# Opening a two-block transformer by quarters: an earlier x, columns from PSUM, a moved filler, three weight units rounded ahead

## The reference

```python
cond = jax.nn.silu(c)
mod = (cond @ ada_w[l] + ada_b[l])[:, None, :]
sh1, sc1, g1, sh2, sc2, g2 = jnp.split(mod, 6, axis=-1)
h = rmsnorm(x, norm1_g[l]) * (1 + sc1) + sh1
proj = h @ w_in + b_in
```

## Time and profile before

| | |
|---|---|
| median of 3 runs | 1454.11 us |
| lowest and highest | 1453.11 and 1454.91 us |
| the profiled execution's own time | 1455.57 us |
| its span in the profile | 1453.8 us |
| TensorE busy | 1424.6 us (98%) |
| GpSimd busy | 1209.7 us (83%) |
| ScalarE busy | 758.7 us (52%) |
| VectorE busy | 718.3 us (49%) |
| moved by transfers | 313.35 MB, mean 216 GB/s |

### The profile page before, as it was taken

The page is one execution under the profiler, slowest core; times in us unless marked ns, Lnnn a source line. Parts: engine busy times, 40 slices in busy tenths (PEclk is TensorE's granted clock), DMA queues, the critical chain, the costliest instruction groups (busy, mean ns, idle before and its releaser), DMA issues.

```text
span 1453.8 us, 21473 instructions
## 1 busy us (share of the span) xinstructions
PE 1424.6 (98%) x7560; PEld 1193.2 (82%) x7560; DVE 718.3 (49%) x1555; ACT 758.7 (52%) x1279; POOL 1209.7 (83%) x984
## 2 busy tenths in 40 slices
PE   6999999999999999999999999999999999999997
PEld 4798777799988987778888888878888888788886
DVE  6863654766643754754566303454650044655202
ACT  4435775644444335765654445574654345655442
POOL 3799989898878987559898997967999977789995
PEclk9999999999999999999999999999999999999999
DMA  9994546678875986337675565644555656345561
GB/s 364 401 352 160 198 166 228 237 296 317 311 256 164 401 310 222 109 101 232 215 247 205 188 203 162 200 143 137 195 190 194 222 164 188 131 164 199 193 200 56
DMA packets 147651, 313.35 MB, mean 216 GB/s; under 512 B 11076, under 2 KB 31960, under 8 KB 147544
## 3 DMA queue, kind: packets, MB, share of 16 engines
q1 hardware_dynamic: 145504, 310.55, 62.2%
q10 hardware_dynamic: 2040, 1.42, 0.3%
HBM read 310.87 MB, written 1.06 MB: 215 GB/s over the span
## 4 chain that ended last, share of the span: by engine, by line
PE 86%; POOL 4%; DVE 4%; DMA 2%; ACT 2%; issue 1%; SPq 0%; POOLq 0%; DVEq 0%; ACTq 0%
PE bank L810 54%; PE bank L855 12%; PE bank L856 8%; POOL lo_units L747 4%; PE bank L853 3%; DMA raw_units<-in_w_ffn_out 1%; PE bank L1018 1%; ACT hi_units L1359 1%; PE bank L1002 1%; DMA raw_units<-in_w_ffn_tiles 1%; PE bank L988 1%; PE bank L891 1%; PE bank L1105 1%; PE bank L1034 1%; PE bank L1070 1%
## 5 line engine op out<-in xcount | busy, mean ns | idle before, releaser
L747 POOL TENSOR_TENSOR lo_units<-raw_units,hi_units 128x512 fp32r<-128x512 f32 (+3 forms) x928 | 1150.5, 1275 | 223.3 <-ACT hi_units L1359 222.1
L1359 ACT ACTIVATE hi_units<-raw_units 128x1024 fp32r<-128x1024 f32 (+1 forms) x470 | 482.8, 1030 | 404.7 <-PE bank L810 235.6
L810 PE MATMUL bank<-hi_units,turned 128*128 128x512 f32 (+3 forms) x1600 | 442.2, 391 | 5.9 <-DVE turned L1888 4.3
L810 PEld LDWEIGHTS bank<-hi_units,turned 128*128 128x128 f32 x1600 | 291.7, 189 | 57.7 <-DVE turned L1888 6.3
L856 PE MATMUL bank<-turned,lo_units 128*128 128x256 f32 x1024 | 288.1, 281 | 0.0
L810 PE MATMUL bank<-hi_units,turned_wide 128*128 128x512 f32 x992 | 274.6, 391 | 0.0
L855 PE MATMUL bank<-turned,hi_units 128*128 128x512 f32 x736 | 260.1, 398 | 0.0
L810 PE MATMUL bank<-lo_units,turned 128*128 128x512 f32 (+3 forms) x800 | 253.1, 383 | 0.8 <-POOL lo_units L747 0.5
L810 PEld LDWEIGHTS bank<-hi_units,turned_wide 128*128 128x128 f32 x992 | 185.3, 188 | 38.5 <-issue 0.5
L856 PEld LDWEIGHTS bank<-turned,lo_units 128*128 128x128 f32 x1024 | 194.2, 190 | 0.2
L810 PEld LDWEIGHTS bank<-lo_units,turned 128*128 128x128 f32 x800 | 150.0, 188 | 30.9 <-POOL lo_units L747 3.6
(11 more groups left out here) (256 smaller groups left out, 1288.1 us busy)
## 6 DMA issues: line engine op xcount, KB each, us to landing
ada_units<-in_ada_w SPq DMA_DIRECT2D x72, 512.0 KB, 7.2
raw_units<-in_w_ffn_tiles SPq DMA_DIRECT2D x72, 512.0 KB, 4.7
raw_units<-in_mlp_w_out SPq DMA_DIRECT2D x64, 512.0 KB, 3.2
raw_units<-in_mlp_w_tiles SPq DMA_DIRECT2D x56, 512.0 KB, 3.2
raw_units<-in_w_in SPq DMA_DIRECT2D x56, 458.0 KB, 9.9
raw_units<-in_w_in SPq DMA_DIRECT2D x48, 512.0 KB, 6.8
raw_units<-in_w_ffn_out SPq DMA_DIRECT2D x44, 512.0 KB, 3.8
raw_units<-in_moba_w_qkv SPq DMA_DIRECT2D x24, 512.0 KB, 3.7
```

Source lines behind the costliest of these rows:

```text
L747: pool.tensor_tensor(LO[:, s, b, 0:w], RAW[:, u["slot"], b, 0:w], HI_[:, s, b, 0:w].bitcast(F32), ALU.subtract).then_inc(lo_ready.sem, lo_ ...
L810: ins = pe.matmul(BANK[2 * c["pair"] + t][:, 0:w], (A[a] if A is BT else A[:, a])[:, part, t * P:(t + 1) * P], W[:, s, b, 0:w], start=(i = ...
L1359: act.activation(HI_[:, s, 0:n, 0:w], RAW[:, u["slot"], 0:n, 0:w], ACT.Copy)\
```

## The change

1. SP sends the two halves of x ahead of the unit (0, 0, 2) and not (0, 0, 3).
2. The columns are worked out as sums * gain + bias with one operand in PSUM each time. The gain is 1 for the shift; for the scale it is g, and the bias is (b + 1) * g, which one new operation, `first_constants`, makes from the tables behind the reciprocal on VectorE. The host's table has the gains spread out: 32 numbers to a partition where it was 24.
3. The filler between the turns and the first column sums goes behind them.
4. Behind the loop over the quarters, and ahead of the sine, ScalarE rounds units 8, 9 and 10 (`prep(11)`).

```diff
--- before.py
+++ after.py
@@ -470,8 +470,7 @@
     ZA, ZU, ZL, LF, F8 = (small(NT * HC) for _ in range(5))
     MX, NM, RS, RR = (small(48) for _ in range(4))
     STAT = small(24)
-    FIRST_BIAS, FIRST_GAIN = NM[:, 0:2 * KT], NM[:, 2 * KT:3 * KT]
-    BIASED, GAINED = RS[:, 0:2 * KT], MX[:, 0:KT]
+    FIRST_BIAS, FIRST_GAIN, FIRST_SCALED = NM[:, 0:2 * KT], NM[:, 2 * KT:4 * KT], RS[:, 0:2 * KT]
     MV, RSTD, NMR = small(4), small(2), small(2)
 
     BANK = [ctx.enter_context(nc.psum_tensor(f"bank{i}", [P, CW], F32)) for i in range(8)]
@@ -662,7 +661,7 @@
                     sp.wait_ge(unit_used.sem, unit_used.at(last_unit["branch", l, 1, "B"]))
                 if (l, c, i) == (0, 4, 0):
                     sp.dma_start(CON[:, n_early:n_const], dram["constants"][:, n_early:n_const]).then_inc(late_const_in, 16)
-                if (l, c, i) == (0, 0, 3):
+                if (l, c, i) == (0, 0, 2):
                     for t in range(NT):
                         sp.dma_start(X[:, t, :], dram["x"][0, t * P:(t + 1) * P, :]).then_inc(x_in[t], 16)
                 if (l, c) in FIRST_BANK:
@@ -1218,9 +1217,8 @@
                 ready = lambda g: (act_side, ("unit rows", g // 2))
                 turn(tag, O, range(4), 0, ready)
                 turn(tag, O, range(4), 1, ready)
-                keep_running(1, BANK[3])
                 column_sums(0)
-                keep_running(1, BANK[3])
+                keep_running(2, BANK[3])
                 for q in range(N_FIRST):
                     pe.wait_ge(turned_lo.sem, turned_lo.at((tag, q)))
                     unit(c0, q, HT)
@@ -1382,7 +1380,8 @@
             bank = BANK[(TQ, TP)[q % 2]]
             for k in (0, 1):
                 part = bank[:, k * S:(k + 1) * S]
-                ins = act.activation(part, part, ACT.Identity, scale=GAINED[:, 2 * q + k:2 * q + k + 1], bias=BIASED[:, 4 * q + 2 + k:4 * q + 3 + k])
+                ins = act.activation(part, part, ACT.Identity, scale=FIRST_SCALED[:, 4 * q + k:4 * q + k + 1],
+                                     bias=FIRST_SCALED[:, 4 * q + 2 + k:4 * q + 3 + k])
             ins.then_inc(act_side.sem, act_side.mark(("whole", q)))
             act.wait_ge(act_side.sem, act_side.at(("whole", q)))
             act.activation(HT[:, 2 * q:2 * q + 2, 0, :], bank[:, :].rearrange("p (k s) -> p k s", k=2), ACT.Copy)\
@@ -1652,7 +1651,7 @@
         act.dma_start(CON[:, 0:n_early], dram["constants"][:, 0:n_early]).then_inc(const_in, 16)
         act.wait_ge(c_in, 16)
         act.activation(CT, COND, ACT.Tanh, scale=0.5).then_inc(act_side.sem, act_side.mark("cond"))
-        act.dma_start(NM[:, 0:3 * KT], dram["first_columns"]).then_inc(first_in, 16)
+        act.dma_start(NM[:, 0:4 * KT], dram["first_columns"]).then_inc(first_in, 16)
         act.dma_start(RB[:, :], dram["rel_bias"].rearrange("l h r -> (l h) r")).then_inc(rel_in, 16)
         act.dma_start(POS[:, :], dram["positions"].rearrange("b (t p) -> (b p) t", p=P),
                       allow_slow_non_contiguous=True).then_inc(pos_in, 16)
@@ -1674,6 +1673,7 @@
                     if q == 0:
                         unit_rows(1)
                     prep(2 * q + 2)
+                prep(2 * N_FIRST + 3)
                 for what, dst in (("sin", SIN), ("cos", COS)):
                     act.wait_ge(rows.sem, rows.at(what))
                     act.activation(dst, dst, ACT.Sin).then_inc(act_side.sem, act_side.mark(what))
@@ -1931,12 +1931,17 @@
 
         def first_columns(q):
 
-            dve.wait_ge(first_in, 16)
             dve.wait_ge(product.sem, product.at(("columns", q)))
             cols = slice(4 * q, 4 * q + 4)
-            link(v.tensor_tensor(BIASED[:, cols], BANK[SB_[1]][:, cols], FIRST_BIAS[:, cols], ALU.add))
-            say(v.scalar_tensor_tensor(GAINED[:, 2 * q:2 * q + 2], BIASED[:, 4 * q:4 * q + 2], 1.0, FIRST_GAIN[:, 2 * q:2 * q + 2], ALU.add, ALU.mult),
-                ("columns", q))
+            sums = BANK[SB_[1]][:, cols]
+            link(v.tensor_tensor(sums, sums, FIRST_GAIN[:, cols], ALU.mult))
+            say(v.tensor_tensor(FIRST_SCALED[:, cols], sums, FIRST_BIAS[:, cols], ALU.add), ("columns", q))
+
+        def first_constants():
+
+            dve.wait_ge(first_in, 16)
+            scales = lambda a: a.rearrange("p (q four) -> p q four", q=N_FIRST)[:, :, 0:2]
+            link(v.scalar_tensor_tensor(scales(FIRST_BIAS), scales(FIRST_BIAS), 1.0, scales(FIRST_GAIN), ALU.add, ALU.mult))
 
         def across_norm(take, norm, next_tag):
 
@@ -2087,6 +2092,7 @@
             first_sum(0, kt)
         dve.wait_ge(act_side.sem, act_side.at(("root", ("n1", 0))))
         say(v.reciprocal(RR[:, 0:NT], RSTD), "inverse root")
+        first_constants()
         for kt in range(6, KT):
             first_sum(0, kt)
         for l in range(DEPTH):
@@ -2591,7 +2597,9 @@
     half = CW // 2
     cols = [np.concatenate([np.arange(D + q * half, D + (q + 1) * half), np.arange(q * half, (q + 1) * half)]) for q in range(N_FIRST)]
     first = np.stack([w[:, c].reshape(P, KT, CW) for c in cols])
-    columns = np.concatenate([b[c].reshape(4, P) for c in cols] + [g.reshape(KT, P)]).T
+    ones = np.ones((2, P), g.dtype)
+    gains = [np.concatenate([g.reshape(N_FIRST, 2, P)[q], ones]) for q in range(N_FIRST)]
+    columns = np.concatenate([b[c].reshape(4, P) for c in cols] + gains).T
     return {"in_ada_first": np.ascontiguousarray(first), "in_first_columns": np.ascontiguousarray(columns)}
 
 
```

## The result

The changed kernel takes a median of **1458.74 us** over 8 runs (1457.41 to 1459.40), the kernel before 1453.94 over 8 (1453.11 to 1454.91). The ratio is 1.0032, with an interval of 1.0021 to 1.0043: slower by 4.8 us, where 4.8 had been predicted. The profiled execution took 1458.59 us, its span 1456.8.

The account below looks back on a forecast made before the run. TensorE was taken to bound the kernel, with 86% of the chain of waits. The terms -1.45 + 5.4 - 0.55 + 1.4 gave +4.8 us on a median of 1454.11: 1458.9 us predicted, range 1453.0 to 1461.0 (the case's own 1456.5 to 1461.0).

Parts of the forecast that it names:

- x and the first constants: Opening: x one transfer sooner gains 0 (at worst 0.3 us lost); the added operation behind the reciprocal costs 0.
- The cover: Before the seventh sum: its 0.40 us wait for a transfer was to hide the added operation's 0.18 us.
- The opening: Filler moved and columns reworked: first columns 1.30 us sooner, 0.15 in the next quarter, -1.45 us; worse bound -0.9.
- the step: Filler and columns: ScalarE starts the first columns at 17.4 instead of 18.70, after unit 0's rounding.
- Six more operations held: VectorE before the first projection's drain: GpSimd's eight subtractions hold six more small operations, +5.4 us (3.6 to 6.3).
- The two short delays: Around unit 8: 0.30 us from drain end to its start and about 0.25 us for its low part go, -0.55 us.
- The half clock at unit 8: TensorE idles 6.3 us before unit 8, then runs at half clock: +1.4 us, between 0 and twice that.
- a shift at 55 us reaches the end unchanged: From 55 us on: TensorE passes on what the opening gains or loses, carried to the end unchanged.
- VectorE is held: Against the rival at L2064 to L2081 that VectorE is not held up further: 1452.1 or 1451.2 us, chance 0.13.
- GpSimd does not pause: Against the rival that GpSimd pauses as unit 9 or 10 is rounded later: +1.3 us, 1455.4, chance 0.09.
- VectorE does get its turn: Against the rival that VectorE waits at L2056 until 53.4: +1.5 us on top, 1460.4, chance 0.04.

Follow-up runs that it names:

- e4: The changed kernel without units 8 to 10 rounded ahead and with x back at its old place; 1452.24 us, 0.9983 of the kernel before.
- e1: The changed kernel with units 8 to 10 rounded after the sines again, so the opening alone; 1452.74 us, 0.9988 of the kernel before.
- e2: The kernel before with units 8 to 10 rounded ahead and nothing else; 1461.91 us, 1.0047 of the kernel before.
- e6: The changed kernel with one unit (8) rounded ahead of the sines instead of three; 1453.85 us, 1.0004 of the kernel before.
- e3: The changed kernel with the angles and most of what follows in a free PSUM bank; 1451.21 us, 0.9978 of the kernel before.
- e9: The changed kernel with five matmuls of no use on TensorE between units 7 and 8; 1456.73 us, 1.0020 of the kernel before.

## Why the prediction was right

**x and the first constants, 0:** right, by e4 and by the reciprocal in the timeline after. The cover that I had counted on for the first constants was not there: the transfer of the seventh sum had landed at 12.34, so the operation at 12.87 put that sum off by 0.2 us. It cost nothing because the column sums (15.19) stood behind the turns and not behind the last sum, which was done at 14.62.

**The opening, -1.45:** the direction was right and the size too small. The trace has -2.55 (unit 7's first subtraction at 43.16, before at 45.71), e1 -1.84 (43.87). Two things lie in this. Unit 0 landed at 15.45 in the profiled execution of after and at 16.36 in that of before, and I had taken unit 0's rounding, which follows it, as the limit of the first columns. In e1, where it landed at 16.48, they started at 17.38, and the step says 17.4. At the first columns the gain is 2.05 us in the trace of after, where I had 1.30. The rest is mostly the clock, which I had put into the bounds as a possible loss. In the two executions with the old opening TensorE rested 2.96 and 2.70 us before unit 0, and the clock was at half from 20.62 to 24.03 and, in e2, from 18.82 to 25.64. In the eleven others it rested 1.15 to 2.02 us and the clock stayed up there. At half clock TensorE comes late to the second quarter's column sums. From the timeline of the kernel before:

```profile
24.32 0.75 DVE L1926 SCALAR_TENSOR_TENSOR mod_rows<-ada_units,small,bank 128x512 f32<-128x512 f32 x1
...
25.51 0.95 PE L1200 MATMUL bank<-ones_rounded,mod_rows 128*128 128x1 f32 x8
```

The sums' input is done at 25.07, and they start 0.44 us later; in the kernel after it is 0.05 us (23.02 and 23.07). In e2, where unit 0 landed at 15.36, the gain of the early landing was lost again in this way:

```profile
22.62 1.73 PE L810 MATMUL bank<-hi_units,turned 128*128 128x458 f32 x4
...
23.31 0.75 DVE L1927 SCALAR_TENSOR_TENSOR mod_rows<-ada_units,small,bank 128x512 f32<-128x512 f32 x1
...
25.71 0.95 PE L1200 MATMUL bank<-ones_rounded,mod_rows 128*128 128x1 f32 x8
```

Here the input is done at 24.06, and the sums start at 25.71. That the shorter rest is what kept the clock is argued from these thirteen executions and not shown; no kernel changed the rest alone. Against it speaks a later rest: TensorE waits 1.18 or 1.19 us for the last quarter's column sums in all thirteen, near 40 us, and in six of them, the kernel after and e2 among them, the clock fell at 39.83 to 42.71, in the other seven not.

**Six more operations held, +5.4:** right. 10.19 in place of 4.85 us from the first subtraction to the drain is +5.34, and e2 and e6 bear the count out: by GpSimd's instructions, as long as VectorE's operations run from SBUF to SBUF. In e3, where most of them don't, ten instructions of GpSimd hold two.

**The two short delays, -0.55:** right. From the drain's start to unit 8 it is 1.23 us instead of 1.54, and before, unit 8 took 0.33 more than the 2.77 of e6, its wait for the low part: -0.64.

**The half clock at unit 8, +1.4:** right. Unit 8 took 4.39 us in place of 2.77: +1.62.

**The sum.** -2.55 + 5.34 - 0.64 + 1.62 = +3.77 at unit 9, where I had +4.8; the medians differ by 4.8, and their interval goes from 3.1 to 6.3. So the time came out closer than the sum behind it, whose opening was too small by 1.1 us, and that is luck. The two profiled executions differ by only 3.0 us (1458.59, where I had put the like of 1455.57 at 1460.4), and no run shows where the last microsecond between +3.77 and the medians lies. That a shift at 55 us reaches the end unchanged holds in these two traces to some 450 us and not beyond. The measured parts, -1.7 (e1) and +7.4 (e2), give +5.7. e2 came out worse than expected, at unit 9 by +7.49 for +6.2, by a longer half clock behind the drain: it was at 0.50 from 56.36 to 63.19, and units 8 and 9 took 7.99 us together, in the kernel after 6.89.

**The rivals.** None came true. VectorE is held; GpSimd does not pause (unit 10 landed at 46.89, and it wanted it at 49.98); and VectorE does get its turn.

## What to carry to other kernels

Work that is moved earlier on one engine starts its consumers earlier too: look at what these then meet, here GpSimd's subtractions against fourteen tiny VectorE operations on the way to a drain. Where tiny SBUF-to-SBUF operations on VectorE must run beside a busy GpSimd, put an operand or the result of each into PSUM, or move them into a gap. With that the same rounding ahead cost nothing: e3 and e1 lie 1.5 us apart in one batch (1451.21 and 1452.74), of which the trace shows 0.6 us at unit 8. The PSUM operands without the rounding ahead were not run.

## What was not expected of the hardware

The same transfer lands at different times from one execution to the next: unit 0 at 15.29 to 16.48 us in thirteen, whatever the order of x. And how long TensorE rests did not settle what its clock does: it stayed up after 2.63 us in e6 and fell a microsecond after work had resumed in e9, where the rest was 1.96, and after one and the same rest near 40 us it fell in six executions of thirteen.
